# Running the later stages of a hybrid decoder's first pass one block of tokens at a time

## What is computed

```python
proj = x @ w_in                       # z, xbc, dt, u, v and two gates
y_a = ssd_branch(z, xbc, dt, ...)     # causal conv, chunked scan over the tokens, norm
y_b = chunk_sgu_branch(u, v, ...)     # gelu, layer norm of v, mix inside 128 tokens
merged = sigmoid(g_a) * (y_a @ w_branch_a) + sigmoid(g_b) * (y_b @ w_branch_b)
h = layer_norm(ALPHA * x + merged @ w_out)
...
q = h @ w_q                           # 8 heads, two halves each
s = q . sub_keys                      # 128 scores for each half
cand = top16(s_first) + top16(s_second)   # 16 x 16 sums, of these the best 16
expert, gate = indices, softmax(best)     # 8 heads x 16 = 128 experts for each token
act = gelu(h . u_tab[expert])
out = sum(gate * act * v_tab[expert])     # a row of 2048 floats from each table
y = layer_norm(ALPHA * h + out)
```

## Time and profile before

| | |
|---|---|
| median of 3 runs | 5205.01 us (5204.82 to 5212.57) |
| span of the profiled execution | 5205.6 us |
| PE / DVE / POOL / ACT busy | 4523.2 / 2803.0 / 2236.7 / 858.0 us |
| moved by DMA | 1674.51 MB, mean 322 GB/s |
| first pass (first weight matmul to the start of the second pass) | 32.0 to 1820.1 us |
| second pass | 1820.1 to 3809.6 us |
| tail | 3809.6 to 5205.6 us |

### The profile page before, as it was taken

The page is one execution under the profiler, slowest core; times in us unless marked ns, Lnnn a source line. Parts: engine busy times, 40 slices in busy tenths (PEclk is TensorE's granted clock), DMA queues, the critical chain, the costliest instruction groups (busy, mean ns, idle before and its releaser), DMA issues. The chain is left out here.

```text
span 5205.6 us, 48526 instructions
## 1 busy us (share of the span) xinstructions
PE 4523.2 (87%) x18494; PEld 3370.4 (65%) x18494; DVE 2803.0 (54%) x3713; ACT 858.0 (16%) x1941; POOL 2236.7 (43%) x1647
## 2 busy tenths in 40 slices
PE   8999999999999897897789798999857777887776
PEld 6888878888887686776677687787733332332222
DVE  4565622000002678898866665666876655364445
ACT  2333311100000133333301110000111111110000
POOL 3676640000000345454533523455578875364442
PEclk9999999999999998998899899999978899899999
DMA  6766664445554499999999899999999999999998
GB/s 204 228 212 218 199 194 130 139 147 165 165 187 123 125 390 397 417 417 408 403 364 394 338 416 398 397 417 417 376 383 422 421 422 419 382 400 422 421 421 368
DMA packets 331808, 1674.51 MB, mean 322 GB/s; under 512 B 47201, under 2 KB 62113, under 8 KB 195873
## 3 DMA queue, kind: packets, MB, share of 16 engines
q0 software_dynamic: 160640, 1133.71, 53.3%
q1 hardware_dynamic: 165768, 536.51, 30.0%
q10 hardware_dynamic: 5168, 1.19, 0.1%
HBM read 1633.31 MB, written 37.89 MB: 321 GB/s over the span
## 5 line engine op out<-in xcount | busy, mean ns | idle before, releaser
L584 PE MATMUL psum<-rows_a,w_ring 128*128 128x264 f32 x6656 | 1499.2, 387 | 13.7 <-PEq L539 8.9
L584 PEld LDWEIGHTS psum<-rows_a,w_ring 128*128 128x128 f32 x6656 | 1263.3, 191 | 233.9 <-issue 19.0
L584 PE MATMUL psum<-x_and_spare,w_ring 128*128 128x256 f32 x5632 | 1263.6, 385 | 81.9 <-PEq L539 69.1
L584 PEld LDWEIGHTS psum<-x_and_spare,w_ring 128*128 128x128 f32 x5632 | 1080.3, 193 | 251.6 <-issue 92.8
L392 POOL DMA_INDIRECT rows_a<-in_peer_u,expert x384 | 723.7, 1885 | 922.7 <-DVE rows_a L447 857.6
L447 DVE SCALAR_TENSOR_TENSOR rows_a<-rows_a,h_tokens 128x2048 f32<-128x2048 f32 x388 | 889.0, 2293 | 366.4 <-DMA rows_a<-in_peer_u,expert 305.5
L392 POOL DMA_INDIRECT rows_a<-in_peer_v,expert x382 | 506.5, 1326 | 375.6 <-PE psum L491 167.6
L491 PE MATMUL psum<-rows_b,diags 128*128 128x512 f32 x1008 | 483.6, 629 | 193.9 <-ACT diags L481 147.7
L491 PE MATMUL psum<-rows_a,diags 128*128 128x512 f32 x1008 | 488.8, 635 | 149.5 <-ACT diags L481 101.7
L491 PEld LDWEIGHTS psum<-rows_b,diags 128*128 128x128 f32 x1008 | 194.0, 200 | 482.5 <-issue 296.9
L491 PEld LDWEIGHTS psum<-rows_a,diags 128*128 128x128 f32 x1008 | 195.9, 202 | 441.7 <-issue 301.1
(11 more groups left out here) (372 smaller groups left out, 3385.7 us busy)
## 6 DMA issues: line engine op xcount, KB each, us to landing
w_ring<-in_w_tiles SPq DMA_DIRECT2D x896, 512.0 KB
rows_a<-in_state_ssm POOLq DMA_DIRECT2D x32, 512.0 KB, 5.7
out_ssm_sample<-rows_a POOLq DMA_DIRECT2D x32, 512.0 KB, 5.5
rows_a<-acum_rows_dram SPq DMA_DIRECT2D x16, 512.0 KB, 5.0
rows_a<-smp_bc_dram POOLq DMA_DIRECT2D x8, 1024.0 KB, 8.3
acts_by_token<-late SPq DMA_DIRECT2D x16, 512.0 KB, 6.7
branch_b<-acum_rows_dram SPq DMA_DIRECT2D x16, 512.0 KB, 7.5
rows_a<-in_xT SPq DMA_DIRECT2D x3, 2048.0 KB, 18.1
```

The lines of the kernel that those rows point to most:

```text
L584: last = pe.matmul(o, w[:, k * P:(k + 1) * P], x[:, k, :], start=start and k == 0, stop=stop and k == KB - 1)
```

## The change

The first pass is cut behind `sgu`. A `Front` is ssd and sgu of two blocks as before; a `Back` is the rest. There are two fronts and three backs: back a has block 0 (128 columns), back b has block 1 and the samples (136 columns), back c has blocks 2 and 3 (256 columns). The order is front 0, back a, back b, front 1, back c, tail. So the 112 tiles of `back` are streamed three times, not twice. Back a loads whole tiles (8 KB in a row). Back b has experts' steps 0 to 31 inside it. The first pass's heads are kept as scores, with two chosen in each q stage, the other six of block 0 in back b's gates and those of block 1 in front 1's scan. The scan's output and the branch_b activations are stored per back, and x is loaded for each back.

```diff
-PASS_CHUNKS = ((0, 2), (2, 2))
...
-RINGS = (3, 3)
...
+FRONT_CHUNKS = ((0, 2), (2, 2))
+BACK_CHUNKS = ((0, 1), (1, 1), (2, 2))
+BACKS_OF = ((0, 1), (2,))
+RING = 3
+STREAM, WHOLE = [], []
+for _backs in BACKS_OF:
+    STREAM += ORDER[:O_GATE]
+    WHOLE += [False] * O_GATE
+    for _b in _backs:
+        STREAM += ORDER[O_GATE:]
+        WHOLE += [_b == 0] * (N_TILES - O_GATE)
...
-STEPS_B = (13, 20, 16, 32, 15, 32, 16, 3, 18)
+STEPS_B = (8, 4, 8, 4, 4, 4)
+STEPS_F = (10, 15, 18)
+STEPS_C = (30, 15, 29, 15, 3, 19)
...
+            if WHOLE[q]:
+                if q >= RING:
+                    sp.wait_ge(self.w_used, q - RING + 1)
+                sp.dma_start(slot, tile).then_inc(self.w_in[q % RING][0], 16)
...
+        back("b", *STEPS_B)
+        scan, v, u = STEPS_F
+        for g in range(G):
+            put("f1", [("ssd", g, c) for c in range(9)], scan)
+        put("f1", tiles("v", FT), v)
+        put("f1", tiles("u", FT), u)
+        back("c", *STEPS_C)
...
+        heads = [(1, p) for p in range(EARLY, PH)] if ex else []
+        choose_at = {(i, 2): i for i in range(len(heads))}
+        share_at = {(i, 6): i for i in range(len(heads))}
...
+                    if (g, c) in choose_at:
+                        i = choose_at[g, c]
+                        act.wait_ge(ranked, i + 1)
...
+        late = [(0, p) for p in range(EARLY, PH)] if ps.smp else []
+        late_at = {2 + 5 * i: i for i in range(len(late))}
+        late_share = {c + 3: i for c, i in late_at.items()}
...
+                if ps.smp:
+                    for s in range(4):
+                        ex.u_row(pool, s)
+                    for s in range(4):
+                        ex.v_row(pool, s)
...
+                if ps.i == 0:
+                    two = self.backs[1]
+                    sp.dma_start(xs_next[:, :, 0:two.np],
+                                 a["xT"][:, :, two.first:two.first + two.np]).then_inc(self.xb_in, 16)
...
-                for m in range(0 if pick else FT):
-                    p, s = m // 2, m % 2
-                    dve.wait_ge(scored, m + 1)
```

More of the change, by code:

```diff
@@ L704, in first_pass @@
             late = flat(rows_a)[:, KB * ps.n:KB * (ps.n + TP - ps.np)].rearrange("p (k t) -> p k t", k=KB)
+            yb_two = sb("branch_b_two", [P, KB * P + 2 * two.n])[:]
+            own = self.region(flat(rows_a)[:, 2 * every:])
+            own = [own(KB, one.n) for _ in range(3)]
             self.make = self.tables(xs, late)
             self.smp = Samples(self, cut, sb)
-            self.one_pass(ps, xs, spare, yb, m_acts, None)
-    def later_pass(self, ps, ex):
+            kept = self.kept[:]
@@ new lines, in first_pass @@
+            by_tile = lambda x, n: x[:, 0:KB * n].rearrange("p (k t) -> p k t", k=KB)
+            gated = [by_tile(yb, ps.n)[:, :, 0:one.n], by_tile(yb_two, two.n)]
+            self.stage(lambda st: self.ssd(st, ps, xs, spare, yb, m_acts, None))
+            self.stage(lambda st: self.sgu(st, ps, xs, spare, yb, m_acts, gated, None))
+            xs_two = by_tile(flat(self.htok[:, CH - 2:CH, :]), two.n)
+            self.stage(lambda st: self.back(st, one, xs[:, :, 0:one.n], own, gated[0], yb, self.late[:], spare, kept,
+                                            xs_two, None))
@@ L711, in later_pass @@
+            self.stage(lambda st: self.back(st, two, xs_two, (xs_two, gated[1], xs_two), gated[1], yb_two,
+                                            self.late[:], spare, kept, None, ex))
+    def later_pass(self, ps, three, ex):
         with ExitStack() as st:
-            sb = lambda name, shape: st.enter_context(self.nc.sbuf_tensor(f"{name}{ps.i}", shape, F32))[:]
+            sb = lambda name, shape: st.enter_context(self.nc.sbuf_tensor(f"{name}_{ps.name}", shape, F32))[:]
             xs = self.region(self.shared[:])(KB, ps.n)
@@ new lines, in later_pass, with stage @@
+            gated = [self.region(yb)(KB, ps.n)]
+            kept = self.region(self.late[:])(2 * PH, ps.n)
+            self.stage(lambda st: self.ssd(st, ps, xs, spare, yb, m_acts, ex))
+            self.stage(lambda st: self.sgu(st, ps, xs, spare, yb, m_acts, gated, ex))
+            self.stage(lambda st: self.back(st, three, xs, (xs, gated[0], xs), gated[0], yb, m_acts, spare, kept,
+                                            None, ex))
+    def stage(self, build):
+        with ExitStack() as st:
+            build(st)
+        self.clear_sems()
@@ L1763, in _, with share @@
+                def share(i, b, p):
+                    pool.wait_ge(inverted, i + 1)
+                    top.shares(pool, i, self.gates[:, b:b + 1, TOPK * p:TOPK * (p + 1)]).then_inc(self.gate_done, 1)
+                if ps.smp:
+                    for s in range(4):
+                        ex.u_row(pool, s)
+                    for s in range(4):
+                        ex.v_row(pool, s)
                 for c in range(2 * FT):
-                    if pick and c == 2:
+                    if ps.last and c == 2:
@@ L1935, in experts, with choose, invert @@
                         ex.step(dve, s)
+                def choose(i, p):
+                    if i >= 1:
+                        dve.wait_ge(matched, i)
+                    top.choose(o, dve, i, [kept[:, 2 * p + s, 0:P] for s in range(2)], ranked, i + 1, picked)
+                def invert(i):
+                    dve.wait_ge(exp_done, i + 1)
+                    top.inverse(dve, i).then_inc(inverted, 1)
                 for c in range(2 * FT):
-                    if pick and c == 2:
+                    if ps.last and c == 2:
                         for s in range(2):
@@ L1988, in _ @@
                 dve.wait_ge(ln["summed"], 1)
-                for m in range(FT if pick else 0):
+                for m in range(FT):
                     p = m // 3 - 1
```

412 lines of the change are left out of this document (218 added, 194 removed).

## The result

| | before | after |
|---|---|---|
| median | 5206.99 us (4 runs) | 5238.01 us (5235.1 to 5245.1, 4 runs) |
| profiled span | 5205.6 us | 5232.3 us |
| moved by DMA | 1674.51 MB | 1795.74 MB |

The ratio is 1.006, with a 95% interval of 1.0046 to 1.0074. The kernel is slower by 0.6%, where I had forecast 0.6% faster.

What follows compares the result with a forecast made beforehand. PE alone bound the first pass's back and DMA was full in the second pass; first pass +76, second scan -73, rest of second pass -32: 5205.6 + 76 - 73 - 32 = 5176.6, forecast 5176 us, range 5110 to 5240.

Steps and rivals of the forecast that it cites:

- The bottleneck before: First pass's back: PE alone binds, with DMA room to spare; second pass and tail: DMA is full.
- The narrow tile: Backs a and b: a weight tile takes 3.56 us at 128 columns and 3.66 at 136, against 7.14 wide.
- The loads between the tiles, back a: Back a: queued x, scan output and key loads delay tiles by 11 us in all, between 0 and 25; back a 428.
- Back b: Back b: DMA binds with 487 us against PE's 441, so 490 us, between 475 and 530.
- Rival 3: Back b: equal queue shares starve the weights, so it takes about 530 us, launch 5216; chance 0.11.
- The barriers: First pass: 7 us from back a to b, 12 from back b to the scan instead of 23.5.
- The scan: Second scan: 680 us for 753.1, a gain of 73, with about half of the old waits kept; bounds 640 and 735.
- rival 2: Second scan: selections cost PE 9 us in each of six groups, scan 735, back b 15 more, launch 5246; chance 0.16.
- The sign: Whole launch: faster if the scan gives back at least the 76 us the first pass costs; faster 0.63, slower 0.22.

Runs made afterwards that it cites:

- both experiments with whole tiles: Against the changed kernel: back b's weights in whole tiles, ratio 1.0095, 5251.1 us; back a's weights in halves instead of whole tiles, ratio 1.0044, 5229.2 us.

## Why the prediction was wrong

**The bottleneck before.** Right. PE alone bound the old first back, and what was taken from the second pass came back there: -73.8 and -23.0 against -80 and -25.

**The narrow tile.** Right: 3.58 us against 3.56, and at 136 columns 3.70 against 3.66 (59.2 us for 16 tiles in the run without steps).

**The loads between the tiles, back a.** The step said 11 us for all of them and that "whole tiles or halves should both keep up". Back a took 439.0 for 428. In halves it took 427.3. The mis-sized term is the whole tiles, which I had put at nothing: 11 us in this run, some 6 in most. It was not for lack of bandwidth, since the rate in q1's busy time was the same, 342 and 341 GB/s. That the fetch of a slot began too late is the reading that both experiments with whole tiles fit; a ring with more slots, which would test it, was not run.

**Back b.** This is the step that failed. It took the larger of two floors, DMA's 487 and PE's 441, and added 3. Measured were 518.9. Without a single step the stage already took 470.9, not 441. DMA's 487 supposed the 393 and 414 GB/s of the earlier trace rows, a stretch at a share of 1.00; in back b it was 378 and 386. At my prices the bytes that back b really moved, 121.46 and 68.24 MB, would even have been 474 us. I had checked the prices on the second back of the kernel before, but there a tile has 8.0 us (895.4 / 112), and DMA runs at a share of 0.98 and 397 GB/s. So the stage with both loads came out 7 to 10% above the stage without steps and above DMA's floor. The weights came late: PE waited 35.4 us for them, where the forecast had no such wait. Rival 3 had named this wait and put back b at 530, 11 us off where my 490 was 29 off. Its cause in equal turns between the queues is not shown. Whole tiles left q1's rate as it was or better, and PE waited longer.

**The barriers.** 10.2 and 16.7 for 7 and 12, another 8 us.

**The scan.** 685.2 for 680, but that was luck: two errors cancelled. I had kept half of the old waits (about 50 us) and priced the selections at DVE's busy time. The old waits were nearly gone, and the selections cost 47 us at 13 steps a group; at 10 steps, moving them gained 41. So rival 2 was right in its mechanism: it had 9 us in each of six groups, and the trace has 6.4 to 6.6 in five. It was wrong that this comes on top of the old waits, which holds at 13 steps a group but not at 10: 685.2 for its 735. That its 5246 for the launch is near the 5238 is luck as well, since it had back b at 505. The floors in my sum were off too. DVE was busy for 589.1 us where I had 562. PE at full clock was busy for 630.0 (the edit that moved the selections) where I had 611 from 656.7 times 0.93: the busy time did not fall by as much as the clock had been short.

**The sign.** It was to be decided by whether the second pass gives back what the first costs. It gave back 100 (with the tail), for 105 forecast, and the first cost 126.6 for 76. Of the 56 us between forecast and result back b has 29, back a 11, the barriers 8, the scan with v and u 6. With back b at 490 alone the span would have been 5203, no change from before; the other terms had to be right too for my 5176.

What stays open is why the weights in back b come late, in 24 of the 48 us that 32 steps cost: too little look-ahead with three slots, or too little room on the DMA engines. A ring with a fourth slot would tell it; it was not run.

## What to carry to other kernels

When work moves from a full stage into one with room, price the receiving stage at the pace that it will have with both loads, not at the larger of two floors. In the one stage measured here, with floors of 474 to 487 us by DMA and 471 without the new work, the time was 7 to 10% above them. A new block of work in an engine's program should stand where that engine waits already. Six selections moved from ahead of a conv to behind DVE's work for a chunk, where it waits for PE, gave back 41 us, and moving only the engine that showed the wait made it worse. What the selections still cost at the new place was not measured. When tiles become half as long, the ring has half the time to look ahead, and here fetching in halves was worth more than large packets.

## What I had not expected of the hardware

A DMA share of 0.96 was 367 GB/s in back b and 0.98 was 397 GB/s in the second back of the kernel before: the share alone does not tell that the engines are at their limit. The rate of queue q1 in its own busy time, with the same rows of 4 KB, was 310 GB/s at a share of 0.50 (the old first back), 341 at 0.84 (back a in halves), 378 at 0.96 (back b) and 393 at 1.00. So a price read in a full stage is too low for one that is not full. And PE's clock rose with less waiting: the same scan with the selections moved ran at 1.00 for 0.97, with 630.0 us of PE's busy time for 640.1.
